# Hybrid streaming block: how the spatial weights of branch A are loaded and turned

## What is computed

```python
def _gmlp_mixer(za, v_gain, w_spatial, b_spatial):
    u, v = jnp.split(za, 2, axis=-1)
    v = _rms_norm(v, v_gain)
    vb = v.reshape(Bsz, S // A_BLOCK, A_BLOCK, A_GROUPS, HEAD_DIM)
    i = np.arange(A_BLOCK)                    # A_BLOCK = 128, CHUNK = 64
    mask = (i[:, None] // CHUNK >= i[None, :] // CHUNK).astype(np.float32)
    w = w_spatial * jnp.asarray(mask, dtype=w_spatial.dtype)
    s = jnp.einsum('gij,bnjgc->bnigc', w, vb) + b_spatial.T[None, None, :, :, None]
    return u * s.reshape(Bsz, S, A_WIDTH)
...
def _hybrid_layer(...):
    z = jnp.einsum('bsd,de->bse', _rms_norm(x, norm_mix), w_in)
    ya, yb, yc, yd = (the four mixers on parts of z)
    merged = gates[:, :, 0] * (ya @ a_w_out) + ...      # four gated branches
    x = x + merged @ w_o
    gate, up = jnp.split(_rms_norm(x, norm_ffn) @ w_gate_up, 2, axis=-1)
    return x + (jax.nn.silu(gate) * up) @ w_down
```

## Time and profile before

| | |
|---|---|
| median of 3 runs | 799.5 us (798.94 to 800.38) |
| the profiled execution | 799.06 us |
| its span | 797.2 us |
| TensorE busy | 791.5 us (99%) |
| VectorE busy | 570.7 us (72%) |
| ScalarE busy | 404.6 us (51%) |
| GpSimd busy | 67.9 us (9%) |
| DMA queue of SP | 57.9% of 16 engines' span |

### The profile page before, as it was taken

The page is one execution under the profiler, slowest core; times in us unless marked ns, Lnnn a source line. Parts: engine busy times, 40 slices in busy tenths (PEclk is TensorE's granted clock), DMA queues, the critical chain, the costliest instruction groups (busy, mean ns, idle before and its releaser), DMA issues.

```text
span 797.2 us, 10273 instructions
## 1 busy us (share of the span) xinstructions
PE 791.5 (99%) x3792; PEld 650.2 (82%) x3792; DVE 570.7 (72%) x852; ACT 404.6 (51%) x541; POOL 67.9 (9%) x121
## 2 busy tenths in 40 slices
PE   8999999999999999999999999999999999999998
PEld 6888787878888888888888877887788888888886
DVE  7888988877585756656678778798675757656563
ACT  6865646554264443543476556465542644543431
POOL 5944000000000000000006100000000000000000
PEclk9999999999999999999999999999999999999999
DMA  8664536545466767676673625474446566675651
GB/s 306 200 195 140 169 134 226 192 148 180 133 226 186 228 215 219 194 225 190 187 254 116 228 83 185 141 255 159 159 159 199 169 209 206 232 226 183 215 183 53
DMA packets 112353, 149.64 MB, mean 188 GB/s; under 512 B 14248, under 2 KB 75440, under 8 KB 112304
## 3 DMA queue, kind: packets, MB, share of 16 engines
q1 hardware_dynamic: 112304, 148.98, 57.9%
HBM read 142.54 MB, written 1.05 MB: 180 GB/s over the span
## 4 chain that ended last, share of the span: by engine, by line
PE 95%; POOL 3%; DMA 1%; SPq 0%; DVE 0%; issue 0%; POOLq 0%; DVEq 0%
PE big L1695 20%; PE big L1699 19%; PE big L1698 19%; PE mix L1695 10%; PE mix L1699 10%; PE mix L1698 10%; PE mix L1739 1%; PE mix L1838 1%; PE mix L1763 1%; DMA pos_i<-in_positions 1%; PE mix L1751 1%; PE mix L1785 1%; PE mix L1820 1%; POOL logits L766 1%; POOL rstd L728 0%; POOL logits L768 0%
## 5 line engine op out<-in xcount | busy, mean ns | idle before, releaser
L859 ACT ACTIVATE w_hi<-w_raw 128x2048 fp32r<-128x2048 f32 (+2 forms) x140 | 254.8, 1826 | 174.5 <-DMA w_raw<-in_w_gate_up 89.9
L1183 DVE TENSOR_TENSOR w_lo<-w_raw,w_hi 128x2048 fp32r<-128x2048 f32 (+3 forms) x142 | 305.9, 2161 | 46.6 <-ACT w_hi L859 44.5
L1695 PE MATMUL big<-w_hi,act_hi 128*128 128x512 f32 (+2 forms) x476 | 184.3, 387 | 0.4 <-DVE w_lo L1183 0.4
L1699 PE MATMUL big<-w_hi,act_lo 128*128 128x512 f32 (+2 forms) x476 | 181.5, 381 | 0.0
L1698 PE MATMUL big<-w_lo,act_hi 128*128 128x512 f32 (+2 forms) x476 | 181.4, 381 | 0.0
L1695 PE MATMUL mix<-w_hi,act_hi 128*128 128x512 f32 x352 | 137.1, 390 | 0.0
L1699 PE MATMUL mix<-w_hi,act_lo 128*128 128x512 f32 x352 | 137.0, 389 | 0.0
L1698 PE MATMUL mix<-w_lo,act_hi 128*128 128x512 f32 x352 | 136.9, 389 | 0.0
L1695 PEld LDWEIGHTS big<-w_hi,act_hi 128*128 128x128 f32 x476 | 89.5, 188 | 19.5 <-issue 2.3
L1699 PEld LDWEIGHTS big<-w_hi,act_lo 128*128 128x128 f32 x476 | 89.5, 188 | 17.1
L1698 PEld LDWEIGHTS big<-w_lo,act_hi 128*128 128x128 f32 x476 | 89.6, 188 | 15.8
(11 more groups left out here) (216 smaller groups left out, 744.8 us busy)
## 6 DMA issues: line engine op xcount, KB each, us to landing
w_raw<-in_w_in SPq DMA_DIRECT2D x44, 1024.0 KB, 5.1
w_raw<-in_w_gate_up SPq DMA_DIRECT2D x88, 512.0 KB, 5.0
w_raw<-in_w_down SPq DMA_DIRECT2D x22, 1024.0 KB, 5.0
w_raw<-in_w_o SPq DMA_DIRECT2D x8, 1024.0 KB, 5.0
probs<-merged SPq DMA_DIRECT2D x160, 32.0 KB, 2.8
w_raw<-in_b_w_out SPq DMA_DIRECT2D x4, 1024.0 KB, 5.9
w_raw<-in_w_in SPq DMA_DIRECT2D x4, 512.0 KB, 3.7
w_raw<-in_a_w_out SPq DMA_DIRECT2D x4, 512.0 KB, 4.1
```

The lines of the kernel that those rows point to most:

```text
L859: nc.scalar.activation(high(u)[:, a:b], arrived(u)[:, a:b], ACT.Copy).then_inc(hi_ready, 1)
L1183: nc.vector.tensor_tensor(low(u)[:, a:b], arrived(u)[:, a:b], high(u)[:, a:b].bitcast(F32), ALU.subtract).then_inc(lo_ready, 1)
L1695: ins = nc.tensor.matmul(dst[:, 0:w], xh, wh, start=first and n == 0, stop=False)
L1699: ins = nc.tensor.matmul(dst[:, 0:w], xl, wh, start=False, stop=end)
```

## The change

The spatial weights come no longer in one DMA with the late parameters, but in sixteen DMAs of 32 partitions x 4 groups x 32 columns, four behind each of loads 9 to 12. Square (a, b) of each group lands at partitions b and columns a, so that a transpose within each 32 x 32 block gives the turned matrix. VectorE does this for all four groups in one instruction in slot 9, after a wait for all sixteen, and then the clearing. TensorE's four transposes, their bank use and ScalarE's copy go away.

```diff
-         ... "wT": 8, ...                                     (PE_AT, and its use of bank 3)
-N_LATE_PARAMS = 10
+N_LATE_PARAMS = 9
+        squares_in = signal("squares_in", 16 * MOVES)
             def load_late_params(l):
                 params = (
-                    (w_sp[:], a_w_spatial[l].rearrange("g i j -> i g j")),
+            def load_squares(l, quarters):
+
+                for a in quarters:
+                    for b in range(QUARTERS):
+                        sp.dma_start(w_sp[quarter(b), :, QUARTER * a:QUARTER * (a + 1)],
+                                     a_w_spatial[l, :, quarter(a), quarter(b)].rearrange("g i j -> i g j")
+                                     ).then_inc(squares_in.sem, 16)
                     if (l, u) == (0, RING + 2):
                         load_late_params(0)
+                    if RING + 4 <= u < RING + 8:
+                        load_squares(l, [u - RING - 4])
@@ scalar, steps
-                if s == PE_AT["wT"]:
-                    drain(l, spatial_t[:], "wT", src=by4(mix[:, mix_bank("wT"), :]))
@@ vector, steps
-                if s == PE_AT["wT"] + 1:
-
-                    dve.wait_ge(*mix_is_drained(l, "wT"))
+                if s == PE_AT["kv"] + 1:
+                    dve.wait_ge(*squares_in.nth(l, 16 * MOVES))
+                    step(l, nc.vector.transpose(spatial_t[:].rearrange("p g (a q) -> p (g a) q", a=QUARTERS),
+                                                w_sp[:].rearrange("p g (a c) -> p (g a) c", a=QUARTERS)))
                     nc.vector.memset(spatial_t[CHUNK:P, :, 0:CHUNK], 0.0).then_inc(wt_masked.sem, 1)
@@ tensor, steps
-                if s == PE_AT["wT"]:
-                    bank = mix_bank("wT")
-                    pe.wait_ge(*late_params_in.nth(l, late_params_in.per_layer))
-                    pe.wait_ge(*mix_is_free(l, "wT"))
-                    for g in range(A_GROUPS):
-                        ins = nc.tensor.transpose(mix[:, bank, g * P:(g + 1) * P], w_sp[:, g, :], ident[:])
-                    ins.then_inc(mix_full[bank].sem, 1)
```

More of the change, by code:

```diff
@@ L151, in main_uses @@
     return uses
-PE_AT = {"latT": 5, "TI": 5, "kv": 8, "wT": 8, "TK": 8, "idx0": 11, "TQ": 11, "idx1": 13, "TC": 17, "TJ": 17,
+PE_AT = {"latT": 5, "TI": 5, "kv": 8, "TK": 8, "idx0": 11, "TQ": 11, "idx1": 13, "TC": 17, "TJ": 17,
          "spatial": 12, "mixed": 12, "yaT": 13, "ydT": 14}
@@ L169, in mixer_uses @@
     uses += [(("latT",), 1), (("TI", 0), 2), (("TI", 1), 3), (("kv",), 0),
-             (("TK", 0), 2), (("wT",), 3), (("idx", 0, 0), 0), (("idx", 0, 1), 1),
+             (("TK", 0), 2), (("idx", 0, 0), 0), (("idx", 0, 1), 1),
              (("TQ", 0), 2), (("TQ", 1), 3), (("spatial",), 1), (("mixed",), 2),
@@ L221 @@
            22: (1, 5, 7), 23: (1, 7, 8)}
-DVE_STEPS = 116
+DVE_STEPS = 117
 QUARTER = 32
```

## The result

| | before | changed |
|---|---|---|
| median | 799.94 us (4 runs) | 812.69 us (811.8 to 814.27, 4 runs) |
| ratio | 1 | 1.017, 95% interval 1.0157 to 1.0182 |
| the profiled execution | 799.06 us | 812.16 us |
| its span | 797.2 us | 810.4 us |
| its mean granted clock | 1.000 | 0.993 |

A forecast was written before the change was run, and what follows sets the result against it. TensorE, busy 791.5 of 797.2 us, was taken as the bound. Late unit 11 costs 4.76 us in layer 0 and 4.74 in layer 1, together 9.5, on the 799.5 median: 809.0 us, range 804.5 to 813.0.

The forecast's parts named there:

- The removed transposes: TensorE's queue: four transposes a layer go, saving 0.43 us a layer, 0.86 us in all.
- the limit of 0.2%: Whole kernel: the smallest difference, 1.6 us, that a measurement was said to tell from no change.
- SP's queue: Load issue on SP: sixteenth square issued 2.3 us after load 12 and landed 6.2 us after load 12's issue.
- The estimate by a read-modify-write below 512 B: Square DMAs: 128 B packets taking twice as long land the last square 0.36 us later, 0.7 us in all; not summed.
- VectorE's wait: VectorE after unit 10's low part: stands still for the squares, 4.1 us in layer 0 and 7.2 in layer 1.
- TensorE's wait: TensorE at the middle of slot 10: two waits of about 5 us for unit 11's low part, no others.
- The sum of the waits: TensorE taking unit 11 late: 4.76 us lost in layer 0, 4.74 in layer 1, together 9.5, transposes' saving inside.
- The sum: Prediction step adding landing, transpose and VectorE's run up to unit 11 in both layers: 9.5 us lost, 809.0 us.
- a rival with a chance of 0.22: TensorE's clock drops to 1.2 GHz after idling: 2.8 us a layer, 814.5 us, or 811.8 with half; chance 0.22.
- The late landing: Last square landing 5.1 us after its own issue, the longest of like-sized moves: 811.4 us.
- The other side: VectorE's wait costs nothing if squares land by 57.5 us in layer 0: 799.8 us, no change; chance 0.06.
- The margin in layer 0: Unit 11: TensorE took it 0.15 us after VectorE was done, called no cover, so VectorE's lateness passes to TensorE.

The follow-up runs named there:

- e3: Changed kernel with VectorE's wait, transpose and clearing moved from slot 9 to slot 11; 797.33 us, ratio 0.9982 to the kernel before.
- e8: Changed kernel with squares behind loads 5 to 8 and VectorE's wait, transpose and clearing in slot 11; 797.64 us, ratio 0.9986.
- e11: As e8, with a layer's sixteen squares brought by four DMAs, one behind each of loads 5 to 8; 797.69 us, ratio 0.9984.
- e6: Kernel before plus sixteen square DMAs a layer behind loads 9 to 12 into a free tile; 798.93 us, ratio 1.0004.
- e9: The changed kernel run again, unedited, on the same chip as e10 and e11; 813.42 us, ratio 1.0174 to the kernel before.
- e10: Repeat of e5 beside e9: changed kernel with eleven unread matmuls in each TensorE wait; 810.12 us, ratio 1.0134.
- e2: Changed kernel with the squares behind loads 5 to 8 instead of 9 to 12; 798.30 us, ratio 0.9991 to the kernel before.
- e4: Changed kernel with the squares behind loads 8 to 11, one load earlier; 800.59 us, ratio 1.0024 to the kernel before.
- e7: Kernel before plus one VectorE transpose of 128x512 in slot 9 into a free tile; 799.27 us, ratio 1.0009.
- e1: Changed kernel plus eight unread 128x256 matmuls on TensorE ahead of unit 11; 811.36 us, ratio 1.0147 to the kernel before.
- e5: As e1, with eleven unread matmuls in place of eight; 809.75 us, ratio 1.0139 to the kernel before.

## Why the prediction was right and wrong

- **The removed transposes**, 0.43 us a layer: held. Load 12 of layer 1 moved by 6.22 where the stretch ahead had moved by 6.66. That 0.86 us is all that can be won stands too: e3, e8 and e11 are 1.1 to 1.4 us below the kernel before, and each interval holds 0.86. But ten runs do tell such a difference from none, against the limit of 0.2% that the prediction set.
- **SP's queue**: the last square 2.3 us behind load 12; it was 2.15 (57.91 less 55.76). The landing 6.2 us after load 12: 6.2 in layer 0, and 6.4 in layer 1 (460.88 less 454.50). The estimate by a read-modify-write below 512 B that the prediction set beside it, 0.36 us later in each layer (the Trainium skill, DMA: Bandwidth & Descriptors, Specifications), is not borne out in layer 0; in layer 1 the landing was 0.2 later than forecast, and no run tells whether the size of the pieces did that. e6 shows no cost of it for the other loads.
- **VectorE's wait**: 4.1 and 7.2 us forecast, 4.18 and 7.39 measured. The transpose took 0.71 where 0.69 was taken, and 0.83 us to the start of the clearing where it was 0.72.
- **TensorE's wait**: 5.2 and about 5 us forecast, 5.1 and 5.2 measured, in the middle of slot 10 in both layers.
- **The sum of the waits**, 9.5 us with the saving inside, measured 10.1. Of the 0.6, 0.3 is load 12's place in layer 0, which went at 55.76 and not 55.44 since TensorE had lost that much in the opening, 0.2 is the landing in layer 1, and in each layer 0.1 more between landing and clearing is nearly offset by TensorE, which took unit 11 0.06 us behind VectorE where 0.15 was summed.
- **The step that failed** is "The sum", where it took TensorE's work behind the wait to go on at the starts of before, and left the fall of the clock to a rival with a chance of 0.22. It fell behind both waits and cost 1.6 and 1.8 us by the traces, 3.3 in e9 against e10. Against that rival I had held the clock's 1.00 in the first slice; that row says nothing of an engine that stops after long work. The rival's mechanism was right; its price, 2.8 us a layer for all 12 matmuls left of unit 11, was above what came, since only seven or eight ran slowly. The late landing alone gives 811.4, half of the clock's price alone 811.8 and both together 814.2, so the range's upper end of 813.0 was a choice between them; that the time came out so near to it is no merit of the sum.
- **The other side**, a wait that costs nothing, needed the squares to land by 57.5 us; they landed at 61.98. e2 and e3 show what it would have taken.
- **The margin in layer 0**: I called it no cover. e4, where VectorE is late by 0.3 us and a transpose and TensorE waits 1.2, bears this out; e7, where no wait shows, does not. It was 0.15 us in the one profile that I read, and 0.57 in e6.

## What to carry to other kernels

A wait in an in-order queue costs what stands behind it: ask who needs the next large piece of that engine, and put the wait behind it. Where DMAs are issued behind a load that itself waits for a place in a ring, they land some time after that place is free (here 6.2 to 6.4 us after that load's issue), however early the data could have been read. And where a change makes TensorE idle for some microseconds, price the clock as well as the wait; here it was a third as much again.

## What I had not expected

- Unread matmuls made the program faster: 3.3 us between e9 and e10.
- In layer 0 of the changed kernel the clock reads 0.99 over the idle stretch from 64 to 69 us and is at the lower level when the work starts; in layer 1 it reads 0.69 over 463 to 468, so it fell sooner after the work stopped. The slow stretch behind was alike: 1.6 and 1.8 us lost.
- In e1, with an idle 2.0 us behind 3.6 us of filling matmuls, the clock came down in layer 1 (just after the work had gone on, three matmuls in), and 2.1 us in layer 0 did not; waits of 1.1 and 1.2 us in e4 and of 0.6 to 1.3 behind the longer filling of e5 and e10 never did. So the length of the last wait alone does not say it (2.0 us did and 2.1 did not), and what decides was not tried.
